# Local attention: scores in two sets of three banks, one bank for transposes, three steps of lag

## The reference

```python
def sink_softmax(s, sink):
    sk = broadcast(sink)                       # one logit per head
    return softmax(concatenate([s, sk]))[..., :-1]

def block_attention(xs):                       # one block of 128 queries
    q_b, k_b, v_b, m_b = xs
    s_ctx = einsum('bqgrd,bkgd->bgrqk', q_b, k_c) * scale     # 256 context keys
    s_loc = einsum('bqgrd,bkgd->bgrqk', q_b, k_b) * scale     # blocks i-1, i, i+1
    s_loc = where(m_b, s_loc, NEG_INF)         # |q - k| <= 128, inside the sequence
    p = sink_softmax(concatenate([s_ctx, s_loc]), sink)
    return einsum(p[..., :n_ctx], v_c) + einsum(p[..., n_ctx:], v_b)
```

## Time and profile before

| | |
|---|---|
| median of 3 runs | 3931.47 us |
| profiled execution | 3929.79 us |
| its span, first to last instruction | 3928.0 us |
| busy PE / DVE / ACT over the span | 3495.8 / 1248.7 / 648.7 us |
| PE products of the attention's transposes, L2006 | 50.5 us, 288 instructions |
| PE products with the values, L2023 | 38.6 us, 144 instructions |
| ACT exp, L2037, both shapes | 46.8 us, 64 instructions |
| DVE reduction, L2068, both shapes | 43.5 us, 32 instructions |

### The profile page before, as it was taken

How to read it: one execution, slowest core, us unless ns; L and a number is a source line. 1 busy time by engine, 2 the same in 40 slices (tenths; PEclk the granted TensorE clock), 3 DMA queues, 4 the chain that set the end, 5 groups by cost and what they waited for, 6 DMA issues and landing times. The chain is left out here.

```text
span 3928.0 us, 33380 instructions
## 1 busy us (share of the span) xinstructions
PE 3495.8 (89%) x13546; PEld 1615.2 (41%) x13546; DVE 1248.7 (32%) x2297; ACT 648.7 (17%) x1380; POOL 0.2 (0%) x4
## 2 busy tenths in 40 slices
PE   7999888999889798999785999999988777899987
PEld 3444443444344343556563333333335443433332
DVE  1110752010372435733645122222233543011112
ACT  1000431000251201101112111111021431111111
POOL 0000000000000000000000000000000000000000
PEclk9999899999999898999877999999999888999999
DMA  3333101333301221102210777677831001699996
GB/s 140 130 154 145 43 22 53 128 129 129 129 1 44 78 86 73 43 10 106 105 49 7 278 280 278 258 277 278 311 114 56 1 1 44 255 368 374 371 379 265
DMA packets 86528, 588.05 MB, mean 150 GB/s; under 512 B 12440, under 2 KB 13371, under 8 KB 15972
## 3 DMA queue, kind: packets, MB, share of 16 engines
q1 hardware_dynamic: 78624, 572.56, 37.6%
q10 hardware_dynamic: 7748, 13.30, 1.0%
HBM read 583.73 MB, written 2.10 MB: 149 GB/s over the span
## 5 line engine op out<-in xcount | busy, mean ns | idle before, releaser
L426 PE MATMUL ps<-mem 128*128 128x512 f32 x1152 | 506.7, 599 | 17.6 <-DVE mem L543 17.6
L1641 PE MATMUL ps<-mem 128*64 128x512 f32 x2048 | 474.9, 606 | 41.6 <-issue 20.2
L426 PEld LDWEIGHTS ps<-mem 128*128 128x128 f32 x1152 | 219.2, 192 | 301.9 <-issue 298.8
L1641 PEld LDWEIGHTS ps<-mem 128*64 128x64 f32 x2048 | 144.4, 138 | 334.4 <-issue 329.1
L998 PE MATMUL ps<-mem 128*128 128x512 f32 (+1 forms) x768 | 254.4, 494 | 7.7 <-ACT mem L852 7.7
L1610 DVE SCALAR_TENSOR_TENSOR mem<-ps,mem 128x512 f32<-128x512 f32 x128 | 96.1, 751 | 406.1 <-PE ps L1570 403.4
L998 PEld LDWEIGHTS ps<-mem 128*128 128x128 f32 x768 | 148.3, 194 | 114.1 <-issue 102.1
L770 PE MATMUL ps<-mem 128*128 128x512 f32 x384 | 167.1, 591 | 0.0
L423 PE MATMUL ps<-mem 128*128 128x512 f32 x384 | 167.0, 594 | 0.0
L1265 PE MATMUL ps<-mem 128*128 128x512 f32 (+1 forms) x384 | 142.1, 531 | 7.3 <-POOLq L173 7.3
L487 ACT ACTIVATE mem<-ps 128x512 f32<-128x512 f32 x48 | 28.7, 597 | 688.0 <-PE ps L426 688.0
(11 more groups left out here) (290 smaller groups left out, 3968.9 us busy)
## 6 DMA issues: line engine op xcount, KB each, us to landing
mem<-in_moe_w SPq DMA_DIRECT2D x384, 1024.0 KB, 6.9
mem<-in_w_in SPq DMA_DIRECT2D x48, 1024.0 KB, 9.0
mem<-in_ada_w SPq DMA_DIRECT2D x48, 1024.0 KB, 6.7
mem<-in_hy_w_in SPq DMA_DIRECT2D x24, 1024.0 KB, 6.5
mem<-in_w_out SPq DMA_DIRECT2D x12, 1024.0 KB, 8.6
mem<-in_k_win_l SPq DMA_DIRECT2D x8, 1024.0 KB, 6.8
mem<-in_hy_w_out SPq DMA_DIRECT2D x8, 1024.0 KB, 5.8
mem<-in_sw_w_in SPq DMA_DIRECT2D x6, 1024.0 KB, 5.9
```

The source lines that it names most:

```text
L426: m = mm(ps[:, j % 4, :], Wc[s][:, k, t * P:(t + 1) * P], HTL[:, k, :], start=(k == 0), stop=(k == KD - 1))
L1641: m = mm(ps[64 * x:64 * x + 64, pair, :], lat(k), w[x][:, k % 4, :], start=(k == 0), stop=(k == KD - 1))
```

## The change

- The scores of a unit lie in one of two sets of three banks, 0 to 2 and 3 to 5, by the parity of the unit. The first two banks of a set hold the first four blocks of head 0 and head 1, the third bank the fifth blocks of both. PE's scores of unit s wait for `probs` of unit s-2.
- All transposes go through bank 6: the four blocks of head 0, then the four blocks of head 1, then the fifth blocks of both. Each waits until the one before has been copied out. ACT copies in two instructions of 512 columns, ahead of the exp of its step; DVE copies the fifth blocks, and PE's first half of the next unit waits for that too (`i_ready`).
- `SLAG` is 3, and there are four buffers of probabilities, each one row of 1280 instead of two of 640.
- PE's step: first half of the transposes of unit s-3, score products of unit s, products with the values every fourth unit, second half of the transposes, the second fifth-block product and the masks (marks `scores`), the fifth blocks' transposes (marks `m_ready`).
- In wide units the reduction and the exp of the fifth blocks are instructions of their own (with one more small comparison and one more small addition on DVE). DVE's fifth-block copy and `evac_o` stay at the end of its step.

The diff of the parts on PE, ACT and DVE:

```diff
--- before.py
+++ after.py
@@ -1833,12 +1833,12 @@
 
         wm = Map(AR_)
         QS_, K2_, VS_, PT_, PP_, OS_ = (wm.take(4096), wm.take(4 * 768), wm.take(6 * 256), wm.take(2 * 2560),
-                                        wm.take(3 * 1280), wm.take(4096))
+                                        wm.take(4 * 1280), wm.take(4096))
         AX_, AP_, MK_, RT2_ = wm.take(1024), wm.take(P), wm.take(512), wm.take(1024)
         assert wm.at <= AR_END
         QS, K2, VS = v(QS_, 8, 512), v(K2_, 4, 768), v(VS_, 6, 256)
         PT = [v(at + i * 2560, 5, 4, P) for at in (PT_, HT_) for i in range(2)]
-        PW = [v(PP_ + i * 1280, 2, 640) for i in range(3)]
+        PW = [v(PP_ + i * 1280, 1280) for i in range(4)]
         OS = v(OS_, 8, 512)
         AXT, APM = v(AX_, 2, 512), v(AP_, P)
         WMASK = half_words(MK_, 4 * P).rearrange("p (a b) -> p a b", b=P)
@@ -1958,60 +1958,80 @@
             return [j - 3] if 3 <= j <= 10 else [j - 4] if 12 <= j <= 15 else []
 
         SU = [(g, i, rp) for g in range(4) for i in range(NQ) for rp in range(2)]
-        SLAG = 2
+        SLAG = 3
 
         def window(i):
 
             return list(range(max(0, i - 1), min(NQ, i + 2)))
 
+        def wide(u):
+
+            return len(window(SU[u][1])) == 3
+
         def fifths(u):
 
-            return sum(1 for _g, i, _r in SU[:u] if len(window(i)) == 3)
+            return sum(1 for x in range(u) if wide(x))
+
+        def score_cell(s, c, block):
+
+            if block < 4:
+                return ps[:, 3 * (s % 2) + c, block * P:(block + 1) * P]
+            return ps[:, 3 * (s % 2) + 2, c * P:(c + 1) * P]
 
         def pe_sw_c(A):
             for s in range(len(SU) + SLAG):
-                if s < len(SU):
-                    g, i, rp = SU[s]
-                    if s:
-                        A.e.wait_ge(S["probs"], s)
-                    w = window(i)
-                    lo = TC + w[0] * P
-                    q = [QS[64 * c:64 * c + 64, 2 * g + rp, i * P:(i + 1) * P] for c in range(2)]
-                    k = [K2[64 * c:64 * c + 64, g, :] for c in range(2)]
-                    for c in range(2):
-                        mm(ps[:, 2 * c, 0:TC], q[c], k[c][:, 0:TC], start=True, stop=True)
-                    for c in range(2):
-                        mm(ps[:, 2 * c, TC:512], q[c], k[c][:, lo:lo + 256], start=True, stop=False)
-                    if len(w) == 3:
-                        for c in range(2):
-                            mm(ps[:, 2 * c + 1, 0:P], q[c], k[c][:, lo + 256:lo + 384], start=True, stop=False)
-                    masked = [(x, 3 if kb < i else 2) for x, kb in enumerate(w) if kb != i]
-                    for c in range(2):
-                        for x, msk in masked:
-                            bb, cc = (2 * c, TC + x * P) if x < 2 else (2 * c + 1, 0)
-                            m = mm(ps[:, bb, cc:cc + P], IDB, WMASK[:, msk, :], start=False, stop=True)
-                    m.then_inc(A.mark("scores"), 1)
-                if s >= SLAG:
-                    u = s - SLAG
-                    g, i, rp = SU[u]
-                    nk = 2 + len(window(i))
+                u = s - SLAG
+                if u >= 0:
                     if u:
-                        A.e.wait_ge(S["turned_out"], u)
+                        A.e.wait_ge(S["turned_out"], 2 * u)
                     if fifths(u):
                         A.e.wait_ge(S["i_ready"], fifths(u))
                     A.e.wait_ge(S["weights"], u + 1)
+                    pe_sw_turn(A, u, 0)
+                if s < len(SU):
+                    g, i, rp = SU[s]
+                    if s >= 2:
+                        A.e.wait_ge(S["probs"], s - 1)
+                    q = [QS[64 * c:64 * c + 64, 2 * g + rp, i * P:(i + 1) * P] for c in range(2)]
+                    k = [K2[64 * c:64 * c + 64, g, :] for c in range(2)]
+                    lo = TC + window(i)[0] * P
                     for c in range(2):
-                        for j in range(nk):
-                            o = ps[:, 4 + c, j * P:(j + 1) * P] if j < 4 else ps[:, 6, c * P:(c + 1) * P]
-                            m = tr(o, PW[u % 3][:, c, j * P:(j + 1) * P], IDENT)
-                    m.then_inc(A.mark("turned"), 1)
-                    if u % 4 == 0 and u:
-                        pe_sw_pv(A, u // 4 - 1)
+                        mm(ps[:, 3 * (s % 2) + c, 0:TC], q[c], k[c][:, 0:TC], start=True, stop=True)
+                    for c in range(2):
+                        mm(ps[:, 3 * (s % 2) + c, TC:512], q[c], k[c][:, lo:lo + 256], start=True, stop=False)
+                    if wide(s):
+                        mm(score_cell(s, 0, 4), q[0], k[0][:, lo + 256:lo + 384], start=True, stop=False)
+                        mm(score_cell(s, 0, 4), IDB, WMASK[:, 2, :], start=False, stop=True).then_inc(A.mark("j_ready"), 1)
+                if u >= 4 and u % 4 == 0:
+                    pe_sw_pv(A, u // 4 - 1)
+                if u >= 0:
+                    A.e.wait_ge(S["turned_out"], 2 * u + 1)
+                    pe_sw_turn(A, u, 1)
+                if s < len(SU):
+                    if wide(s):
+                        A.e.wait_ge(S["j_ready"], fifths(s + 1))
+                        mm(score_cell(s, 1, 4), q[1], k[1][:, lo + 256:lo + 384], start=True, stop=False)
+                        mm(score_cell(s, 1, 4), IDB, WMASK[:, 2, :], start=False, stop=True)
+                    masked = [(x, 3 if kb < i else 2) for x, kb in enumerate(window(i)) if kb != i and x < 2]
+                    for c in range(2):
+                        for x, msk in masked:
+                            m = mm(score_cell(s, c, 2 + x), IDB, WMASK[:, msk, :], start=False, stop=True)
+                    m.then_inc(A.mark("scores"), 1)
+                if u >= 0 and wide(u):
+                    A.e.wait_ge(S["turned_out"], 2 * u + 2)
+                    for c in range(2):
+                        m = tr(ps[:, 6, c * P:(c + 1) * P], PW[u % 4][:, 640 * c + 512:640 * c + 640], IDENT)
+                    m.then_inc(A.mark("m_ready"), 1)
             pe_sw_pv(A, len(SU) // 4 - 1)
             end_phase(A)
 
+        def pe_sw_turn(A, u, c):
+            for j in range(4):
+                m = tr(ps[:, 6, j * P:(j + 1) * P], PW[u % 4][:, 640 * c + j * P:640 * c + (j + 1) * P], IDENT)
+            m.then_inc(A.mark("turned"), 1)
+
         def pe_sw_pv(A, w):
-            A.e.wait_ge(S["turned_out"], 4 * (w + 1))
+            A.e.wait_ge(S["turned_out"], 8 * (w + 1))
             A.e.wait_ge(S["i_ready"], fifths(4 * (w + 1)))
             if w:
                 A.e.wait_ge(S["o_out"], w)
@@ -2026,26 +2046,29 @@
 
         def act_sw_c(A):
             for s in range(len(SU) + SLAG):
+                u = s - SLAG
+                for c in range(2):
+                    if u >= 0:
+                        g, i, rp = SU[u]
+                        A.e.wait_ge(S["turned"], 2 * u + c + 1)
+                        if u % 4 == 0 and u >= 8 and c == 0:
+                            A.e.wait_ge(S["o_full"], u // 4 - 1)
+                        act(PT[u // 2 % 4][:, 0:4, 2 * rp + c, :], ps[:, 6, :].rearrange("p (j q) -> p j q", q=P), ACT.Copy)\
+                            .then_inc(A.mark("turned_out"), 1)
                 if s < len(SU):
-                    g, i, rp = SU[s]
-                    wd = (2 + len(window(i))) * P
                     A.e.wait_ge(S["maxima"], s + 1)
-                    if s >= 3:
-                        A.e.wait_ge(S["turned"], s - 2)
+                    if s >= 4:
+                        A.e.wait_ge(S["turned"], 2 * (s - 3))
+                        if fifths(s - 3):
+                            A.e.wait_ge(S["m_ready"], fifths(s - 3))
                     at = 2 * (s % 4)
                     for c in range(2):
-                        act(PW[s % 3][:, c, 0:wd], ps[:, 2 * c:2 * c + 2, :].rearrange("p a n -> p (a n)")[:, 0:wd], ACT.Exp,
+                        act(PW[s % 4][:, 640 * c:640 * c + 512], ps[:, 3 * (s % 2) + c, :], ACT.Exp,
                             bias=MISC[:, 32 + at + c:33 + at + c], accum_out=MISC[:, 40 + at + c:41 + at + c]).then_inc(A.mark(), 1)
+                        if wide(s):
+                            act(PW[s % 4][:, 640 * c + 512:640 * c + 640], score_cell(s, c, 4), ACT.Exp,
+                                bias=MISC[:, 32 + at + c:33 + at + c], accum_out=MISC[:, 56 + at + c:57 + at + c]).then_inc(A.mark(), 1)
                     act(MISC[:, 48 + at:50 + at], MISC[:, 48 + at:50 + at], ACT.Exp).then_inc(A.mark("probs"), 1)
-                if s >= SLAG:
-                    u = s - SLAG
-                    g, i, rp = SU[u]
-                    gi = u // 2
-                    A.e.wait_ge(S["turned"], u + 1)
-                    if u % 4 == 0 and u >= 8:
-                        A.e.wait_ge(S["o_full"], u // 4 - 1)
-                    act(PT[gi % 4][:, 0:4, 2 * rp:2 * rp + 2, :].rearrange("p j c q -> p c j q"),
```

(36 more changed lines are left out.)

## The result

The changed kernel takes 3971.61 us (median of 4 runs, 3967.18 to 3973.27) against 3930.99 us in the runs beside it: ratio 1.010, 95% interval 1.0083 to 1.0118, slower by 41 us. The forecast was 3953 us with a range to 3978: the direction and the mechanism were right, the loss was nearly twice the 22 us of the sum. The profiled execution took 3973.27 us, 43.5 above the one of before.

The account below looks back on a forecast made before the run. The attention phase, a loop of waits through PE, DVE and ACT, was taken to bound the kernel. Its steps at +20.0 us and drain at +2.2 gave +22 on 3929.8: 3952, beside the median 3953 us, range 3934 to 3978.

Parts of the forecast that it names:

- The phase is a loop of waits: Attention phase: no engine or bandwidth is full, and time saved or lost there reaches the end one to one.
- Two sets alone don't open the loop: Masks still wait through ACT's copy queued behind exp; narrow interval 4.7 high / 5.4 low clock, before 5.1 / 6.3 us.
- The fifth-block wait decides: PE's next first transposes wait for DVE's late fifth-block copy in four steps of eight; eight steps 56.5 us, +7.6.
- Prices of the split instructions and halves: Wide units: 256-column reduction 0.45 us, 128-column exp 0.36; ACT's 512-column copy of half the transposes 0.60.
- T, S, PV and tail: PE pieces, high/low clock: four transposes 0.43/0.80 us, scores 1.07/2.01, value products 4.45, first mask to reduction (wide) 0.60/0.92.
- 0->1: Interval between reductions of units 0 and 1 modulo 8, others named likewise; forecast 5.45 high / 7.25 low clock, us.
- The point between the clocks: Eight steps 51.5 high / 62.8 low clock; 0.44 of the way, as in the kernel before, gives 56.5 us.
- The rival with the low clock: Whole phase at the low clock, after pauses ahead of exposed transposes and scores: +46 us, 3977; chance 0.15.
- the likeliest case: The forecast itself: fifth-block wait binds, clock between the levels; 3953 us, own range 3940 to 3968, chance 0.65.
- PE's share of busy time falls: Argument against the rival that the clock stays high throughout the attention phase (+3 us, 3935, chance 0.10).
- Drain: End of the attention phase: three units instead of two, turned and copied in halves; 12.5 us against 10.3.
- the first rival: Fifth-block wait does not bind; eight steps 45.1 high / 52.6 low clock, about -7 us, 3925; chance 0.10.

## Why the prediction was right, and where its size failed

- *The phase is a loop of waits and passes one to one to the end*: right. The issue of the weight loads moved by 43.0 us, the span by 43.5.
- *Two sets alone don't open the loop, because the masks stand behind ACT's in-order copy*: right. With the fifth-block waits gone and the masks late it is 54.5; moving the masks took 10.2 us more off per eight steps, and 8.2 with the waits in place. Both times the clock rose too (0.74 to 0.89, 0.75 to 0.79).
- *The fifth-block wait decides, at s mod 8 = 5, 6, 7, 0*: right, and causal. Copy starts at 2.72, 3.05 and 3.58 after the reduction (forecast 2.72, 3.05, 3.74). Taking the wait away gives back 6.3 to 7.4 us per eight steps, not all 13: it was about half of the loss.
- *Prices of the split instructions and halves*: right within 0.04 us; the fixed part of an instruction that the sum took from the rows of before held. (For the reduction these rows give 0.16 fixed and 0.42 in all, where the sum wrote 0.19 and 0.45; it measured 0.415.) In 4->5 ACT's copy of the first half is done at 4.91, where the sum had 5.08.
- *T, S, PV and tail exposed behind it*: right in order. But the pieces were priced too low at either clock. T followed by S is 1.02 at the low clock, not 0.80, and 0.56 at the high one, not 0.43: half of eight transposes in a row left out the gap at the change of shape, which the timeline shows as 0.33 and 0.17 us of idle time of the weight loads. The new wide tail is 1.27 and 0.80, not 0.92 and 0.60. So 0->1, 1->2, 4->5 and 5->6 lie above even the low-clock column, and 7->0 and 2->3, at a granted clock of 1.00, lie 0.2 and 0.6 above the high one. In 1->2 the path is also another: at the low clock PE works through its queue without a pause, and ACT's loop isn't what it waits for.
- *The point between the clocks*: the other term that failed, and the reason why it could. I took 0.44 of the way for all intervals, the old kernel's place. Eight steps measured 61.4 against 51.5 and 62.8, which looks like 0.9 of the way, but two of the eight intervals ran at the high clock. If each interval is taken from the column of the level that its rows show, the forecast's own prices give 58 to 59: 2->3 and 7->0 high (7.0 and 5.45), 0->1, 1->2, 4->5 and 5->6 low (7.25, 5.4, 6.8 and 8.3), 3->4 and 6->7 in part (6.4 to 6.8 and 11.5 to 12.0). So of the 4.9 us that a steady cycle is above 56.5, about 2 are the level and about 3 the prices above. The rival with the low clock (3977) was much nearer in number than the likeliest case, but by luck in part: its condition, all intervals low, was not met. It is luck too that the kernel with busy products takes 56.8 per eight steps, the forecast's 56.5: it ran at 0.87 and not at 0.82.
- *"PE's share of busy time falls"*, the argument against a high clock: wrong as it stands, since the share went from 0.70 to 0.71. The same pieces at the low clock take longer and count as busy.
- *Drain*: 14.3, not 12.5. It ran at the low clock (four transposes in 1.11 us), but that was priced at 13.5; 0.8 us stay without a term.

In all, the sum was 21 us short: 16 in 24 steps, 3 at the ends of the phase, 2 in the drain. The -7 us of the first rival were never reached: without the wait the loop stands at 54.5, above even the 52.6 of that rival's low-clock sum. It had 6->7 at 6.5 us, and that interval is 9.1 there.

The change can pay, but not as it stands. The second set of scores needs the masks ahead of the wait on ACT, and the fifth blocks need a bank that nobody's next step waits for. With both, and DVE's copy moved up, the kernel beats the one before by 0.6 to 1.2%; masks early and the other bank alone were not run.

What stays open: what exactly brings the clock down in one interval and not in another. Fewer and shorter pauses of PE raised it (0.75 to 0.87 with the busy products), so the pauses are a cause. But 7->0 and 0->1 have the same pause and different levels, so something else counts as well, most likely the work ahead of the pause; no run varies that alone. Nor was the change taken apart: `SLAG` of 3 and the fourth buffer, priced at nothing, have no run of their own.

## What to carry to other kernels

A second buffer opens a loop only if nothing that marks it ready stands, in its own engine's order, behind a wait on the engine that it was to run ahead of: walk each engine's queue, not the data. When several pieces share one bank in turn, the slowest reader's place in its queue (here a 0.42 us copy behind 1.2 us of normalising) becomes part of the period. And don't price PE's pieces at a mean between two clocks: take the level interval by interval, from what PE did ahead of it and in the pause, and take a piece's price from a place where the same piece follows.

## What the hardware showed that was not expected

- Five useless products of 512 columns in each of 16 pauses (0.25 us each at the high clock, nearly twice that in one pause of four) made the changed kernel 23 us faster, the granted clock of the phase going from 0.75 to 0.87; in 6->7, S took 1.07 instead of 2.01 us.
- After the same pause of 2.26 us PE came back at the high clock in 7->0 and at the low one in 0->1, in every steady cycle.
- Two kernels with different orders on PE, the changed one and the one with the value products behind the masks, have the same steady eight steps of 61.42 us, each repeating to within 0.04 us, though single intervals differ by up to 3.9 us. Whether that is chance was not tried.
- The releaser "issue" of the waits table hid 41.9 us of waits for another engine; the timeline showed that DVE's copy ended 0.10 us ahead of each.
